# Two narrow products of a two-block transformer kernel: block compression by 64-row tiles, and the modulation's sums over partitions by column tiles

## The chip, the cores and the metric

The kernel runs on one core of a Trainium2 chip. The core has five engines with an instruction stream each: TensorE (matmuls), VectorE, ScalarE, GpSimd and SyncE, which here issues nearly all DMAs. The metric is the device time of one launch in microseconds, as the median of several runs.

## The reference, cut to what matters

A sequence of 256 tokens of 1024 channels goes through two layers with a feed-forward part of 16384 experts each, and then through one more block with a modulation and sparse attention. All is float32. Two places matter here.

The third block's modulation is six vectors of 1024 numbers, made from one vector c, so it can be worked out at any time before that block begins:

```python
mod = jax.nn.silu(c) @ ada_w[layer] + ada_b[layer]          # (1, 1024) @ (1024, 6144)
shift1, scale1, gate1, shift2, scale2, gate2 = jnp.split(mod, 6, axis=-1)
u = rms_norm_2(h, norm1_g[layer]) * (1 + scale1) + shift1
```

In its attention, keys and values (two kv heads of 64 channels) are compressed: 15 overlapping blocks of 32 tokens each become one row, through a weight of 2048 x 64 that both heads share.

```python
blk = src[:, idx] + pos[None, None, :, None, :]             # 15 blocks of 32 tokens
blk = blk.transpose(0, 1, 3, 2, 4).reshape(B, nc, NSA_KV_HEADS, CMP_BLOCK * HEAD_DIM)
return jax.nn.silu(blk @ w1) @ w2                           # w1 (2048, 64), w2 (64, 64)
```

The expert part of each layer picks 16 experts for each of 8 heads and token; its second half sums the picked rows of `v` by their gates, here as a dense product of all 16384 rows with coefficients that are mostly zero.

## The kernel before, in words

Each engine's instruction stream is written out by a Python function per stage (`..._sp`, `..._po`, `..._ac`, `..._ve`, `..._pe` for SyncE, GpSimd, ScalarE, VectorE and TensorE), and each engine runs its stream in order. There are five stages: `even`, `peer(0)`, `odd`, `peer(1)` and `last`. Waits name an event (`wait_ge("ada", pc, 3)`), and a small class turns them into semaphore values. PSUM is `PS`, 8 banks of 128 partitions x 512 floats. `emptied[b]` holds the event after which bank b may be written again, and `bank_wait(pe, b)` waits for it. All calls of a kind go through one helper, so every matmul shows as line 170 of the profile, every ScalarE activation as 181, and SBUF tensors mostly carry the name `mem`, since they are slices of one large tensor.

Most weights are split into a rounded high part and a low remainder: ScalarE rounds (`hi`, the rows `r_sh<-mem`), VectorE subtracts (`lo`, `r_sl<-mem,r_sh`), and TensorE makes the products with both. These products have rounded operands and take one instruction each. Products of unrounded float32 operands, the ones of this change among them, take two instructions on TensorE.

The second half of an expert part is a loop over 128 blocks `V[j]` of 128 experts. For each block, TensorE makes twelve products of 512 moving columns into banks 4 to 7. ScalarE rounds the coefficients of block j + 1 (`coef_high`) and its weights (`hi`), VectorE makes the remainders, and SyncE loads tiles of 128 x 1024 into four buffers `raw`. In `peer(0)` alone this loop carries the modulation as well: `ada_w` comes in 12 pieces of 512 columns with four loads each. In the blocks j = 4 + 10 pc + 0, 2, 4, 6 VectorE adds the eight products of `silu(c)` with the rows of piece pc into `ada_sum`, 128 partitions x 512. In block 4 + 10 pc + 8 TensorE sums over the partitions (`modulation_pe`): four products whose weights are 128 columns of `ada_sum` and whose moving operand is one column of ones, so that the 512 sums come out as four columns of 128 partitions. In the next such block VectorE adds the biases and stores them in `mod` (event `mod`).

The stage `last` begins on VectorE with the scales `gs1` and `gs2` from `mod`. TensorE first makes `bias_mm`, a table of relative biases, which ScalarE copies out and SyncE sends to device memory and back; then it makes the input projection block by block (`block_T`, `parts_R`). The first normalized activations reach it by way of a Ln and an Exp on ScalarE and of VectorE's products. After twelve blocks (`N1 + N0`) comes `compress(0)` for the keys, then the groups of the projection for the values of the attention (`parts_R`), and between them `compress(1)` for the values. In `blk` the partitions 0 to 63 hold the channels of kv head 0 and 64 to 127 those of head 1. The weight `cw1` comes as 32 tiles of 128 x 128 with the head's 64 x 64 on the diagonal and zeros elsewhere, so that one product over 128 partitions makes both heads' 64 columns:

```python
for i in range(32):
    m = pe.matmul(PS[0:15, 3 - a, 0:128], blk[:, a, i, :], wi[:, i, :], i == 0, i == 31)
```

ScalarE then applies Silu to the 15 x 128 of each a, and TensorE turns them.

## Time and the profile before

| | |
|---|---|
| median of 3 runs | 2443.44 us (2441.01 to 2444.06) |
| span of the profiled execution | 2439.0 us |
| TensorE busy | 2406.4 us, 99% of the span, 16544 instructions |
| VectorE busy | 1712.0 us, 70% |
| ScalarE busy | 1331.9 us, 55% |
| GpSimd busy | 435.7 us, 18% |
| read from HBM | 415.96 MB, 172 GB/s over the span |

The profiled execution's own time is its span, from its first instruction to its last; the runs are timed from outside and lie 2.0 to 5.1 us above it. In rows of a timeline, "x8" is a run of eight instructions of the same kind, the time is from the first one's start to the last one's end, and the bracket says how long the engine stood idle before and what released it. The form `128*128 128x512` of a matmul is the weights' partitions and columns, then the moving operand's. One float32 product appears as two instructions. The ends of matmuls are modelled, so spacing is read from starts.

### The profile page before, as it was taken

Reading aid. Unit: us, or ns where it says so; the run is one execution under the profiler, and the core shown is the slowest. Engines: PE = TensorE matmul, PEld = TensorE weight load, DVE = VectorE, ACT = ScalarE, POOL = GpSimd, SP = SyncE. Lnnn points to the kernel's source line nnn. Section 1 sums busy time; section 2 is a strip of 40 time slices with the busy share of each in tenths; the row PEclk is TensorE's granted clock in tenths of the full one; section 3 lists DMA queues with packets and bytes.
Section 4 is the critical chain, followed back from the end, with each engine's and each line's share of the span. In section 5 each row is a group of like instructions: output and inputs, shape, how many; then the busy total and the mean of one; then the engine's idle time right before and its main releaser. Section 6 shows DMA issues by size and latency. Waiting matters only on the chain.

```text
span 2439.0 us, 41647 instructions
## 1 busy us (share of the span) xinstructions
PE 2406.4 (99%) x16544; PEld 2213.2 (91%) x16544; DVE 1712.0 (70%) x3247; ACT 1331.9 (55%) x2520; POOL 435.7 (18%) x386
## 2 busy tenths in 40 slices
PE   8999999999999999999999999999999999999999
PEld 8899999999888888888999999998888878889999
DVE  7867998678777777656599977775555564636864
ACT  6665445766544444566544466665454554556643
POOL 4700000788200000010000048850000000001000
PEclk9999999999999999999999999999999999999999
DMA  7233555443677787632255544446555564223452
GB/s 280 75 139 114 184 183 182 135 130 130 210 260 255 263 263 263 247 129 97 99 187 182 183 155 131 130 139 211 195 192 195 192 235 173 104 99 144 173 180 80
DMA packets 93200, 421.82 MB, mean 173 GB/s; under 512 B 10296, under 2 KB 12880, under 8 KB 85072
## 3 DMA queue, kind: packets, MB, share of 16 engines
q1 hardware_dynamic: 92720, 418.82, 50.3%
q8 instruction: 133, 2.18, 0.4%
q14 instruction: 59, 0.48, 0.1%
q10 hardware_dynamic: 288, 0.34, 0.0%
HBM read 415.96 MB, written 3.16 MB: 172 GB/s over the span
## 4 chain that ended last, share of the span: by engine, by line
PE 94%; DVE 3%; ACT 3%; issue 1%; DMA 0%; ACTq 0%; DVEq 0%
PE PS L170 93%; ACT mem L181 1%; ACT r_sh L181 1%; DVE r_sl L191 1%; DVE mem L191 1%; PE PS L173 1%; DVE mem L199 0%; ACT L188 0%; DMA mem<-in_v 0%; DMA cst<-in_cst 0%; DVE mem L211 0%; ACT xT L181 0%; ACT r_hhi L181 0%; ACT L181 0%; DVE xT L191 0%
## 5 line engine op out<-in xcount | busy, mean ns | idle before, releaser
L191 DVE TENSOR_TENSOR r_sl<-mem,r_sh 128x1024 fp32r<-128x1024 f32 (+2 forms) x750 | 895.3, 1194 | 521.5 <-ACT r_sh L181 520.6
L181 ACT ACTIVATE r_sh<-mem 128x1024 fp32r<-128x1024 f32 (+2 forms) x750 | 768.5, 1025 | 524.0 <-PE PS L170 468.0
L170 PE MATMUL PS<-r_hhi,r_sh 128*128 128x256 f32 (+1 forms) x2832 | 718.7, 291 | 6.2 <-ACT r_sh L181 3.2
L170 PE MATMUL PS<-r_hlo,r_sh 128*128 128x256 f32 (+1 forms) x2704 | 667.7, 284 | 1.3 <-DVE r_hlo L199 1.1
L170 PEld LDWEIGHTS PS<-r_hhi,r_sh 128*128 128x128 f32 (+1 forms) x2832 | 542.1, 191 | 16.2 <-issue 9.6
L170 PEld LDWEIGHTS PS<-r_hlo,r_sh 128*128 128x128 f32 (+1 forms) x2704 | 518.0, 192 | 5.9 <-DVE r_hlo L199 3.3
L196 POOL TENSOR_SCALAR xT<-cst,mem 128x128 f32<-128x128 f32 x256 | 327.4, 1290 | 560.3 <-ACT mem L181 498.0
L170 PE MATMUL PS<-r_hhi,r_sl 128*128 128x256 f32 (+1 forms) x2832 | 401.1, 283 | 0.3 <-DVE r_sl L191 0.3
L181 ACT ACTIVATE mem<-PS 128x256 f32<-128x256 f32 (+25 forms) x558 | 186.0, 341 | 339.6 <-PE PS L170 339.1
L170 PEld LDWEIGHTS PS<-r_hhi,r_sl 128*128 128x128 f32 (+1 forms) x2832 | 366.9, 192 | 0.9 <-DVE r_sl L191 0.5
L170 PE MATMUL PS<-r_sh,r_ch 128*128 128x512 f32 x1024 | 276.8, 391 | 1.2 <-ACT r_sh L181 1.2
L170 PE MATMUL PS<-r_sl,r_ch 128*128 128x512 f32 x1024 | 274.9, 389 | 0.0
L170 PE MATMUL PS<-r_sh,r_cl 128*128 128x512 f32 x1024 | 274.8, 389 | 0.0
L170 PEld LDWEIGHTS PS<-r_sh,r_ch 128*128 128x128 f32 x1024 | 190.8, 188 | 42.1 <-ACT r_sh L181 3.1
L170 PEld LDWEIGHTS PS<-r_sl,r_ch 128*128 128x128 f32 x1024 | 192.2, 188 | 40.3
L170 PEld LDWEIGHTS PS<-r_sh,r_cl 128*128 128x128 f32 x1024 | 192.2, 188 | 40.1
L170 PE MATMUL PS<-mem 64*128 64x128 f32 (+9 forms) x886 | 137.7, 308 | 0.3 <-DVE mem L202 0.2
L170 PE MATMUL PS<-xT 128*128 128x128 f32 x1024 | 130.1, 275 | 4.0 <-DVE xT L191 4.0
L170 PEld LDWEIGHTS PS<-mem 64*128 64x128 f32 (+4 forms) x886 | 106.7, 162 | 28.8 <-issue 12.9
L170 PEld LDWEIGHTS PS<-xT 128*128 128x128 f32 x1024 | 122.8, 192 | 4.3 <-issue 4.3
L191 DVE TENSOR_TENSOR r_cl<-mem,r_ch 128x256 fp32r<-128x256 f32 x256 | 107.1, 418 | 2.6 <-ACT r_ch L181 2.6
L181 ACT ACTIVATE mem<-mem 128x256 f32<-128x256 f32 (+6 forms) x153 | 79.9, 531 | 53.2 <-DVE mem L205 49.3
(169 smaller groups left out, 2649.2 us busy)
## 6 DMA issues: line engine op xcount, KB each, us to landing
mem<-in_u SPq DMA_DIRECT2D x256, 512.0 KB, 3.8
mem<-in_v SPq DMA_DIRECT2D x256, 512.0 KB, 4.4
mem<-in_w SPq DMA_DIRECT2D x16, 2048.0 KB, 8.0
mem<-in_ada SPq DMA_DIRECT2D x48, 512.0 KB, 4.2
mem<-in_in SPq DMA_DIRECT2D x9, 2048.0 KB, 8.9
mem<-in_wq SPq DMA_DIRECT2D x8, 2048.0 KB, 8.4
mem<-in_od_in SPq DMA_DIRECT2D x6, 2048.0 KB, 9.4
mem<-in_ev_in SPq DMA_DIRECT2D x5, 2048.0 KB, 13.1
```

Of the source, the lines that this page charges most:

```text
L170: return self.did(self.e and self.e.matmul(out, lhsT, rhs, start=start, stop=stop, skip_group_check=skip))
L173: return self.did(self.e and self.e.transpose(out, in_, identity))
L181: return self.did(self.e and self.e.activation(out, in_, func, **kw))
L191: return self.did(self.e and self.e.tensor_tensor(out, a, b, op))
L196: return self.did(self.e and self.e.tensor_scalar(out, a, s1, s2, op0, op1))
```

## The change

Modulation: the 12 pieces go four at a time. VectorE keeps the sums of four pieces beside each other, in four quarters of a buffer that is free in this loop (`hTf`). Behind every fourth piece TensorE makes four products, now with one column of ones as the weights and the 512 columns of a piece's sums as the moving operand; each goes to a 32-column tile of its own and leaves a row of 512 sums in partition 0, 32, 64 or 96 of a bank. ScalarE, which took no part before, copies the four rows to SBUF and issues four DMAs that write them to a buffer `md` in device memory. At the end of the loads of `odd`, SyncE loads the 6144 numbers back as 48 rows of 128; TensorE turns them to 128 x 48 as its first instructions of `last`, ahead of `bias_mm`, and VectorE adds all biases in one operation and stores `mod`, ahead of `gs1` and `gs2`. ScalarE waits for its last DMAs in `odd`, before it writes there to the buffer that the rows came from.

Compression: for each i there are two products with 64 partitions and 64 columns, one for each head, into two banks (3 - a and 6 + a), in place of one with 128 partitions and 128 columns. The weights in memory stay as they were; the zeros are no longer read. ScalarE applies Silu to each head's 15 x 64 by itself.

```diff
-    ada_sum = small[:, 0:512]
+    ada_sum = [hTf[:, 512 * i:512 * i + 512] for i in range(4)]
+    ada_row, ada_in = small[:, 0:512], small[0:48, 640:768]
...
                     hi(ac, V[j + 1])
+                if j:
+                    modulation_ac(ac, j - 1)
...
+                s = ada_sum[pc % 4]
                 if q == 0:
                     ve.wait_ge("cs", 0)
-                    if pc:
-                        ve.wait_ge("ada_sum", pc - 1)
-                    d = ve.tensor_scalar(ada_sum, r_[:, 0:512], cs[:, 0:1], MUL)
+                    if pc >= 4:
+                        ve.wait_ge("ada_rows", pc // 4 - 1)
+                    d = ve.tensor_scalar(s, r_[:, 0:512], cs[:, 0:1], MUL)
...
-            else:
-                ve.wait_ge("ada_sum", pc)
-                ve.tensor_tensor(mod[:, 4 * pc:4 * pc + 4], PS[:, pc % 4, 0:4], P("adab")[:, 4 * pc:4 * pc + 4], ADD).then_inc("mod", pc)
+
+        def four_pieces(j):
+
+            pc = (j - 4) // 10
+            if layer or j < 4 or pc >= 12 or pc % 4 != 3 or (j - 4) % 10 != 8:
+                return None
+            return pc // 4
 
         def modulation_pe(pe, j):
-            pc = (j - 4) // 10
-            if layer or j < 4 or pc >= 12 or (j - 4) % 10 != 8:
+            g = four_pieces(j)
+            if g is None:
                 return
-            b = pc % 4
-            bank_wait(pe, b)
-            pe.wait_ge("ada", pc, 3)
+            bank_wait(pe, g)
+            pe.wait_ge("ada", 4 * g + 3, 3)
             for m in range(4):
-                last = pe.matmul(PS[:, b, m:m + 1], ada_sum[:, 128 * m:128 * m + 128], ones[:, 0:1], True, True)
-            last.then_inc("ada_sum", pc)
-            emptied[b] = ("mod", pc)
+                last = pe.matmul(PS[32 * m:32 * m + 1, g, :], ones[:, 0:1], ada_sum[m], True, True)
+            last.then_inc("ada_rows", g)
+            emptied[g] = ("ada_row", g, 3)
+
+        def modulation_ac(ac, j):
+            g = four_pieces(j)
+            if g is None:
+                return
+            ac.wait_ge("ada_rows", g)
+            if g:
+                ac.wait_ge("ada_out", g - 1, 3)
+            for m in range(4):
+                d = ac.activation(ada_row[32 * m:32 * m + 1, :], PS[32 * m:32 * m + 1, g, :], COPY).then_inc("ada_row", g, m)
+            ac.wait_ge(*d)
+            for m in range(4):
+                at = 512 * (4 * g + m)
+                ac.dma_start(io["md"][at:at + 512].rearrange("(o n) -> o n", o=1), ada_row[32 * m:32 * m + 1, :]).then_inc("ada_out", g, m)
...
+            sp.wait_ge("ada_out", 2, 3)
+            sp.dma_start(ada_in, io["md"].rearrange("(m n) -> m n", n=128)).then_inc("ada_in", 0)
...
             hi(ac, ns[1])
+            ac.wait_ge("ada_out", 2, 3)
             scale_ac(ac, 2)
...
-                        ac.activation(hid15[0:15, 128 * a:128 * a + 128], PS[0:15, 3 - a, 0:128], ACT.Silu).then_inc("cmpS", a)
+                        ac.activation(hid15[0:15, 128 * a:128 * a + 64], PS[0:15, 3 - a, 0:64], ACT.Silu)
+                        ac.activation(hid15[0:15, 128 * a + 64:128 * a + 128], PS[0:15, 6 + a, 0:64], ACT.Silu).then_inc("cmpS", a)
...
-            ve.wait_ge("mod", 11)
+            ve.wait_ge("ada_turned", 0)
+            ve.wait_ge(*ve.tensor_tensor(mod, PS[:, 7, 0:48], P("adab"), ADD).then_inc("mod", 0))
...
         def last_pe(pe):
+            bank_wait(pe, 7)
+            pe.wait_ge("ada_in", 0)
+            pe.transpose(PS[:, 7, 0:48], ada_in, ident[0:48, 0:48]).then_inc("ada_turned", 0)
+            emptied[7] = ("mod", 0)
             bank_wait(pe, 6)
...
-                bank_wait(pe, 3 - a)
+                heads = ((slice(0, 64), 3 - a), (slice(64, 128), 6 + a))
+                for _, b in heads:
+                    bank_wait(pe, b)
...
                 for i in range(32):
-                    m = pe.matmul(PS[0:15, 3 - a, 0:128], blk[:, a, i, :], wi[:, i, :], i == 0, i == 31)
+                    for rows, b in heads:
+                        m = pe.matmul(PS[0:15, b, 0:64], blk[rows, a, i, :], wi[rows, i, rows], i == 0, i == 31)
                 m.then_inc("cmp", a)
-                emptied[3 - a] = ("cmpS", a)
+                for _, b in heads:
+                    emptied[b] = ("cmpS", a)
```

## Rows read from the trace of the kernel before

**Rows 1.** The page: busy time of the engines, and the chain by line.

```profile
PE 2406.4 (99%) x16544; PEld 2213.2 (91%) x16544; DVE 1712.0 (70%) x3247; ACT 1331.9 (55%) x2520; POOL 435.7 (18%) x386
...
PE PS L170 93%; ACT mem L181 1%; ACT r_sh L181 1%; DVE r_sl L191 1%; DVE mem L191 1%; PE PS L173 1%; DVE mem L199 0%; ACT L188 0%; DMA mem<-in_v 0%; DMA cst<-in_cst 0%; DVE mem L211 0%; ACT xT L181 0%; ACT r_hhi L181 0%; ACT L181 0%; DVE xT L191 0%
```

**Rows 2.** Windows: length; PE, PEld, DVE, ACT, POOL busy; PEclk, DMA share, GB/s.

```profile
633.87:992.49 358.62, 357.80 (x1622) 296.30 (x1621) 262.83 (x365) 174.83 (x256) 0.00 (x0) 1.00 0.79 265
1631.43:1977.61 346.18, 345.77 (x1527) 285.82 (x1525) 199.25 (x257) 174.92 (x256) 0.00 (x0) 1.00 0.61 202
```

**Rows 3.** Timeline of TensorE, first layer's expert sums: start, length, instruction.

```profile
667.99 1.07 PE L170 MATMUL PS<-r_sh,r_ch 128*128 128x512 f32 x4
...
670.72 0.95 PE L170 MATMUL PS<-cst,small 128*128 128x1 f32 x8
671.53 1.17 PE L170 MATMUL PS<-r_sh,r_ch 128*128 128x512 f32 x4
...
674.38 1.07 PE L170 MATMUL PS<-r_sh,r_ch 128*128 128x512 f32 x4
```

**Rows 4.** Chain of waits in the last stage: start, length, what ran.

```profile
1993.06 52.66 PE PS L170 x379
```

**Rows 5.** Timeline of TensorE, last stage, around both compressions.

```profile
2021.86 1.02 PE L170 MATMUL PS<-mem,cst 128*128 128x512 f32 x2
2022.81 7.16 PE L170 MATMUL PS<-mem 128*15 128x128 f32 x64
2029.90 0.40 PE L170 MATMUL PS<-r_sh,r_hhi 128*128 128x280 f32 x1
...
2034.92 7.16 PE L170 MATMUL PS<-mem 128*15 128x128 f32 x64
```

**Rows 6.** Timeline of TensorE: narrow tiles in the first and last stage.

```profile
42.58 1.71 PE L170 MATMUL PS<-mem 64*128 64x128 f32 x16
...
82.63 0.35 PE L170 MATMUL PS<-mem 64*64 64x128 f32 x4
...
2086.45 0.43 PE L170 MATMUL PS<-mem 128*64 128x256 f32 x2
```

**Rows 7.** Window over the 64x64 tiles, of the tile mem alone.

```profile
82.63:83.07 0.44, 0.44 (x16) 0.44 (x18) 0.44 (x2) 0.44 (x3) 0.44 (x1) 1.00 0.00 0
```

**Rows 8.** Groups by line and form, ScalarE: count, busy us, mean ns, idle before.

```profile
L181 ACT ACTIVATE mem<-PS 128x512 f32<-128x512 f32 x8 | 4.6, 590 | 2.0 <-PE PS L170 2.0
...
L181 ACT ACTIVATE mem<-PS 128x64 f32<-128x64 f32 x6 | 1.3, 216 | 0.0
```

**Rows 9.** Timeline of all engines, start of the last stage.

```profile
1986.06 1.22 DVE L191 TENSOR_TENSOR r_sl<-mem,r_sh 128x1024 fp32r<-128x1024 f32 x1
...
1986.75 0.81 PE L170 MATMUL PS<-cst,small 33*8 33x384 f32 x2
...
1988.10 0.34 SPq L229 DMA_DIRECT2D fd<-mem  x1
...
1988.91 1.35 DVE L199 SCALAR_TENSOR_TENSOR hT<-xT,mem,small 128x256 f32<-128x256 f32 x2 [1.63 <-ACT small L181]
```

**Rows 10.** Timeline of ScalarE, first layer's expert sums.

```profile
670.98 1.06 ACT L181 ACTIVATE r_sh<-mem 128x1024 fp32r<-128x1024 f32 x1 [1.36 <-PE PS L170]
...
688.78 1.06 ACT L181 ACTIVATE r_sh<-mem 128x1024 fp32r<-128x1024 f32 x1 [1.90 <-DMA mem<-in_v]
```

**Rows 11.** Timeline of VectorE and ScalarE around the compressions.

```profile
2023.69 0.68 DVE L202 COPY mem<-PS 128x512 f32<-128x512 f32 x1
...
2039.81 0.48 DVE L226 MEMSET mem<- 128x512 f32 x1 [0.17 <-DVE mem L202]
...
2043.94 1.06 ACT L181 ACTIVATE r_sh<-mem 128x1024 fp32r<-128x1024 f32 x1 [0.25 <-PE PS L170]
...
2045.81 0.33 DVE L202 COPY mem<-PS 128x15 f32<-128x15 f32 x2 [5.51 <-PE PS L170]
```

**Rows 12.** Windows at the last stage's start; columns as in rows 2.

```profile
1992.00:1996.00 4.00, 3.74 (x11) 2.73 (x12) 3.72 (x10) 2.37 (x6) 1.99 (x3) 0.50 1.08 319
```

More of the change, by code:

```diff
@@ L283, in declare @@
     io["fd"] = io["fd_t"].ap()
+    io["md_t"] = nc.dram_tensor("md", (12 * 512,), F32, kind="Internal")
+    io["md"] = io["md_t"].ap()
     io["xs"] = nc.dram_tensor("xs", (128, 2048), F32, kind="Internal").ap()
@@ L1591, in modulation_ve @@
                     ve.wait_ge("ada", pc, q - 1)
-                    d = ve.scalar_tensor_tensor(ada_sum, r_[:, 0:512], cs[:, 2 * q:2 * q + 1], ada_sum, MUL, ADD)
+                    d = ve.scalar_tensor_tensor(s, r_[:, 0:512], cs[:, 2 * q:2 * q + 1], s, MUL, ADD)
                 ve.wait_ge(*d.then_inc("dveC"))
-                ve.scalar_tensor_tensor(ada_sum, r_[:, 512:1024], cs[:, 2 * q + 1:2 * q + 2], ada_sum, MUL, ADD).then_inc("ada", pc, q)
-            else:
-                ve.wait_ge("ada_sum", pc)
-                ve.tensor_tensor(mod[:, 4 * pc:4 * pc + 4], PS[:, pc % 4, 0:4], P("adab")[:, 4 * pc:4 * pc + 4], ADD).then_inc("mod", pc)
+                ve.scalar_tensor_tensor(s, r_[:, 512:1024], cs[:, 2 * q + 1:2 * q + 2], s, MUL, ADD).then_inc("ada", pc, q)
```

## The prediction

> **What bounds the kernel now.** I read the page first. TensorE is busy for 99% of the span, and one line of matmuls holds 93% of the chain that ended last [rows 1]; so time taken out of TensorE's stream counts in full, unless another wait ends later at the same place. Then the two stretches that the change touches. The windows of the two expert-sum loops compare themselves: the first layer's, which carries the modulation, took 358.62 us, the second layer's, the same work without it, 346.18 us, 2.72 us for each step from block to block (127 of them) [rows 2]. TensorE's timeline inside the first shows where the difference sits: the block with the eight one-column products behind it takes 3.54 us (667.99 to 671.53), the next one 2.85 us (671.53 to 674.38) [rows 3]. In the last stage the chain of waits is TensorE alone for 52.66 us from 1993.06 on, and both compressions lie in it [rows 4]. In its timeline the two instructions of 512 columns that begin at 2021.86 (1.02 us with the last one's latency, 0.427 us each) have streamed out at about 2022.71; the first compression starts at 2022.81, the block behind it at 2029.90; the second starts at 2034.92 and is as long [rows 5].
>
> **Modulation, removed.** One piece costs TensorE (3.54 − 2.72) + (2.85 − 2.72) = 0.95 us [rows 2, 3]; 12 pieces are 11.4 us, nearly the 12.4 us by which the loops differ. All of it is path. VectorE's 12 small additions and its waits for them go too; it idles there anyway, so I count nothing.
>
> **Modulation, added.** Three groups, each of four fp32 products with one weight column and 512 moving columns. An fp32 product is two instructions (eight for a piece's four products, [rows 3]), and one of 512 columns streams 0.427 us [rows 5], so one piece is 0.86 us. Whether four such streams run together decides the price. The trace has two narrower cases. With 64x64 tiles, four instructions had started by 82.67, 0.04 us after the first, and by 83.07 sixteen of 128 columns [rows 6, 7]; one at a time they would take 16 x 0.109 = 1.74 us, by the pace of [rows 5]. With 128-row, 64-column tiles, which share all rows as the new ones do, two had started within 0.02 us [rows 6]. Four column tiles over all 128 rows are not in the trace. Bounds: 0.86 us a group (all together) to 3.42 us (in turn). I take 0.86: wherever instructions alternate between tiles, the rows show them side by side. To it come a gap of 0.09 us where the tile shape changes (2022.71 to 2022.81, [rows 5]), once in and once out, and the 0.13 us that the block behind loses today: 1.17 us a group, 3.5 us in all. Saved: 7.9 us (bounds 0.2 and 8.5).
>
> ScalarE gets new work in this loop: after each group a wait, four copies of a 1x512 row out of PSUM and four DMA issues. Copies of 512 columns mean 0.59 us [rows 8]; a DMA issue of like size, on SP, took 0.34 us [rows 9]; with 0.2 us for the wait on its own last copy that is 3.9 us. Queued behind it are its roundings of coefficients and weights for two blocks on, then VectorE's remainder of that tile, then TensorE. The two roundings take 1.37 us a block (174.92 us over 128 blocks, [rows 2]). Counted from the end of the last product ahead of the group: the sums reach ScalarE at 1.15 us (until then it rounds a tile anyway, 1.06, [rows 10]), and TensorE wants the later tile at 1.17 + 2 x 2.72 = 6.6 us. So 6.6 − 1.15 − 1.37 = 4.1 us are free; the cover is ScalarE's idle 1.36 us a block [rows 10] and its lead of one block. 3.9 fits, barely: zero. Without that cover I would pay up to 0.5 us a group, 1.5 us. The weight tiles' DMAs, which already end some of ScalarE's waits (688.78, [rows 10]), are held back by as much at most, and have two blocks without a modulation load to catch up. The 24 KB to device memory and 24 KB back are a tenth of one such tile. Behind the last group five blocks, 13.6 us, of the loop are left before the odd stage waits for its DMAs. The load back is one more issue on SP (0.34 us), behind the attention's output weights and ahead of the next query weights, which wait for freed slots anyway: nothing.
>
> **Compression.** Before: 64 instructions of 128 columns, 7.16 us with the last one's latency, 0.109 us apart; from 2022.71 to 2029.90, with a gap at either end, 7.18 us [rows 5]. After: 128 instructions of 64 columns, by turns two for one head on rows 0 to 63 and two for the other on rows 64 to 127. By 0.427 us for 512 columns, 128 would be 107 ns and 64 be 53; with the 2 ns that 109 has over 107, 0.0555 us. If the two row halves overlap, 64 x 0.0555 = 3.55 us, with gaps 3.73, and 3.45 us are saved each time, 6.9 us in all. If they go in turn, 128 x 0.0555 = 7.1 us, and nothing is. The rows lean to overlap: the 64x64 tiles took sixteen instructions in 0.44 us, 27 ns each, the very rate needed here (two in 55 ns) [rows 7]. Where one row half had all eight instructions ahead of the other's, little overlapped: sixteen took 1.71 us [rows 6]; the new loop alternates after two. What no row shows is that rate for more than 24 instructions; the longest steady run of short ones is the compression itself, 64 at 109 ns. So the bounds of a compression are 3.5 and 128 x 0.109 + 0.18 = 14.1 us; I take 3.73, as the burst is of the same kind.
>
> The burst's 27 ns stands against a rule of the Trainium skill, "TensorE: Matmul & The Clock Gate", section "Back-to-back issue gap": with hardware decoding off about 62 ns a matmul bind where the columns are few, otherwise a floor of about 25 ns. The burst agrees with the floor, but is too short to exclude the other. By the burst the whole sum is the −14.5 us below; by 62 ns, an estimate from that page, a compression would be 128 x 0.062 + 0.18 = 8.1 us and the sum −5.7.
>
> New waits there: banks 6 and 7 must be free of the bias tiles 2 and 3. VectorE copies the last of these out from 2023.69, 0.68 us, the one before it earlier still, ahead of the first compression [rows 11]; tile 3 is wanted by the second, then at about 2031.4. No stall. ScalarE makes four Silu calls of 64 columns (some 0.22 each, [rows 8]) in place of two; behind them it now idles 0.25 us before the next tile, at 2043.94 [rows 11]: that covers the 0.2. Who is late next? VectorE's work behind the head norm ends with a memset at 2039.81 + 0.48; its next wait ends at 2045.81, 5.51 us later [rows 11]. The compression takes 3.45 of these, 2 remain. So 6.9 us arrive.
>
> **Start of the last stage.** The turning of the 48x128 rows stands ahead of the bias matmul, which is on the path: it starts at 1986.75, and by way of ScalarE's copy and scale steps VectorE's first product starts at 1988.91 [rows 9]. Eight instructions with 128 weight columns took 0.95 us with latency, 0.1 each [rows 3]; two of these and a gap: +0.3 us. VectorE adds the biases behind it, two small products, and then its 1.22 us remainder [rows 9]; that ends at about 1989.0, under the delayed 1989.2. Bounds 0.1 and 0.7.
>
> **Sum.** −7.9 − 6.9 + 0.3 = −14.5 us on a span of 2439.0, so 2424.5. The runs' median is 4.4 us above that span (time outside the profiled instructions, or a quick run); I carry that: 2443.4 − 14.5 = 2428.9.
>
> **The clock.** TensorE ran at its half level, 1.2 GHz, through 1992 to 1996, behind the wait at the stage's start [rows 12]. The work behind it moves earlier by 8 to 15 us; one such stretch of 4 us more or less is worth half its length, 2 us, either way.
>
> **The rivals.** *Column tiles of full height go in turn.* For it: no row has four. Against: two do overlap. A group costs 3.42 + 0.31 = 3.73, 11.2 in all; only 0.2 saved: −0.2 − 6.9 + 0.3, 2436.6 us. 7%.
>
> *The row halves of the compression go in turn.* For it: the 1.71 us run. Against: alternating instructions. −7.9 + 0.3: 2435.8 us. 4%.
>
> *Instructions are not handed over fast enough* (the slower end). The place is the compression: twice the instructions, half as long. For it: no lasting rate above one in 109 ns, and the 64x64 burst could have been queued beforehand. Against: 27 ns held for sixteen. At 109 ns a compression takes 14.1 in place of 7.18, and the sum is −7.9 + 13.9 + 0.3 = +6.3: 2449.7 us, 4%. The sign turns at 84 ns (7.6 us over two runs are 3.8, and 3.8 + 7.0 = 10.8 over 128). Half way between the two rates, 68 ns: 8.7 + 0.18 = 8.9, 1.7 more each, −7.9 + 3.4 + 0.3: 2439.2 us, 7%. The skill's 62 ns, quoted above, lies beside it.
>
> *ScalarE's new work holds the loop, or a half-clock stretch is added*: 1.5 + 2 us, 2432.4. 4%.
>
> *Forecast*: 74%, own range 2425 to 2432. The three runs differ by 0.12%, and 0.2% (4.9 us) is about what can be told from no change. Faster than that: the forecast and all rivals but the two of the hand-over, 0.89, less 0.01 for waits that I did not see. Same: the half-way rate and that 0.01, 0.08. Slower: 0.04. Range: from the forecast's low end, 2425, to 2437, which takes in both in-turn cases.
>
> **What would show it.** In the profile after: the first loop's window at about 350.7 us, with three stretches of eight instructions of 512 columns and one weight column, about 0.9 us long; each compression 128 instructions in some 3.7 us; ScalarE's copies of 1x512, and no wait of TensorE for ScalarE two blocks on; the last stage's first block 0.3 us later behind its sums. Wrong if the eight instructions take over 3 us, or if the compression's start 60 ns apart or more.

## The result, and the profile after

The change made the kernel faster: 2426.73 us as the median of 4 runs (2424.63 to 2429.40) against 2442.94 us for the kernel before in the same session, a ratio of 0.9937 with a 95% interval of 0.9926 to 0.9949, or 12.5 to 18.1 us. The same kernel in two more sessions gave 13.5 and 14.9 us less (runs 1 and 12 below). One execution of run 3 (3919.51 us, at a granted clock of 0.556) is left out of that run's numbers. The forecast was 14.5 us less, 2428.9 us.

The profiled execution has a span of 2427.6 us, 11.4 less than before. The page of the profile after, busy time and chain, answers to [rows 1]; TensorE still holds nearly all of it:

```profile
PE 2395.0 (99%) x16601; PEld 2199.7 (91%) x16601; DVE 1712.3 (71%) x3236; ACT 1338.9 (55%) x2534; POOL 436.0 (18%) x386
...
PE PS L170 92%; ACT mem L181 1%; ACT r_sh L181 1%; DVE r_sl L191 1%; DVE mem L191 1%; PE PS L173 1%; DMA mem<-in_v 1%; DVE mem L199 0%; ACT L188 0%; DVE mem L211 0%; DVE hT L199 0%; DMA cst<-in_cst 0%; ACT xT L181 0%; ACT r_hhi L181 0%; ACT L181 0%
```

One share in the second line has risen: a DMA of the expert weights (`in_v`), from 0% to 1% of the chain. The windows of the two expert-sum loops, as in [rows 2]: the first fell from 358.62 to 352.14 us, the second did not move.

```profile
631.78:983.92 352.14, 350.77 (x1550) 285.36 (x1549) 263.24 (x353) 181.50 (x268) 0.00 (x0) 1.00 0.79 270
1624.44:1970.61 346.17, 345.76 (x1526) 285.81 (x1525) 199.24 (x257) 174.92 (x256) 0.00 (x0) 1.00 0.61 202
```

TensorE's timeline around the first of the three groups, as in [rows 3]. The block that begins at 747.83 lasts until 751.61, 3.78 us, and the next 2.85, so a group costs (3.78 − 2.72) + (2.85 − 2.72) = 1.19 us. (The blocks with the second and the third group take 3.91 and 3.92 us in this profile and 3.78 in run 1; before each of them ScalarE had waited for a weight transfer.)

```profile
747.83 1.07 PE L170 MATMUL PS<-r_sh,r_ch 128*128 128x512 f32 x4
...
750.64 1.04 PE L170 MATMUL PS<-hT,cst 128*1 128x512 f32 x8
751.61 1.20 PE L170 MATMUL PS<-r_sh,r_ch 128*128 128x512 f32 x4
...
754.46 1.07 PE L170 MATMUL PS<-r_sh,r_ch 128*128 128x512 f32 x4
```

ScalarE's timeline behind it: four copies, four DMA issues, and two roundings without a pause to catch up:

```profile
751.77 2.42 ACT L181 ACTIVATE small<-PS 1x512 f32<-1x512 f32 x4
754.22 1.35 ACTq L229 DMA_DIRECT2D md<-small  x4
755.62 0.42 ACT L181 ACTIVATE r_ch<-mem 128x256 fp32r<-128x256 f32 x1 [1.43 <-issue]
755.94 1.04 ACT L181 ACTIVATE r_sh<-mem 128x1024 fp32r<-128x1024 f32 x1
```

TensorE's timeline in the last stage, as in [rows 5]: each compression is now 128 instructions, and 3.68 us lie between its first start and the block behind it (2016.54 to 2020.22), where it was 7.09:

```profile
2015.58 1.02 PE L170 MATMUL PS<-mem,cst 128*128 128x512 f32 x2
2016.54 3.75 PE L170 MATMUL PS<-mem 64*15 64x64 f32 x128
2020.22 0.40 PE L170 MATMUL PS<-r_sh,r_hhi 128*128 128x280 f32 x1
...
2025.25 3.75 PE L170 MATMUL PS<-mem 64*15 64x64 f32 x128
```

VectorE's timeline behind the compressions: its wait for TensorE, 5.51 us in [rows 11], is down to 2.11:

```profile
2030.15 0.48 DVE L226 MEMSET mem<- 128x512 f32 x1 [0.17 <-DVE mem L202]
2032.74 0.33 DVE L202 COPY mem<-PS 128x15 f32<-128x15 f32 x2 [2.11 <-PE PS L170]
```

And TensorE's timeline at the last stage's start, as in [rows 9]. From the last block of the second loop to the first block here are 1983.27 − 1970.61 = 12.66 us, against 1990.08 − 1977.61 = 12.47 before: the turning costs 0.19.

```profile
1979.75 0.26 PE L173 MATMUL PS<-cst,small 48*128 48x48 f32 x1
1979.94 0.81 PE L170 MATMUL PS<-cst,small 33*8 33x384 f32 x2
1983.27 0.55 PE L170 MATMUL PS<-r_hhi,r_sh 128*128 128x256 f32 x1 [2.53 <-ACT r_hhi L181]
```

So the profiled execution's 11.4 us come apart as follows. The first loop gave 6.48, the compressions (from the start of the first to the end of the second: 19.20 before, 12.39 after) 6.81, and the last stage's start took 0.19: 13.1 us for the change itself. Where the code is the same, 1.7 us were lost again: 2.09 won ahead of the first loop, and 1.58 lost between the two loops, 0.54 between the last stage's first block and the first compression, and 1.66 behind the second. The first experiment is about these.

### The profile page after: what moved, and what is told of

Read it like the earlier page. It is cut to its first block, busy times and chain, and to the rows that moved or that the text cites. A ratio compares the mean times of both kernels' runs of the same rounds, so it can differ in the third digit from the quotient of the medians.

```text
span 2427.6 us, 41773 instructions
## 1 busy us (share of the span) xinstructions
PE 2395.0 (99%) x16601; PEld 2199.7 (91%) x16601; DVE 1712.3 (71%) x3236; ACT 1338.9 (55%) x2534; POOL 436.0 (18%) x386
## 4 chain that ended last, share of the span: by engine, by line
PE 93%; DVE 3%; ACT 3%; DMA 1%; issue 1%; ACTq 0%; DVEq 0%
PE PS L170 92%; ACT mem L181 1%; ACT r_sh L181 1%; DVE r_sl L191 1%; DVE mem L191 1%; PE PS L173 1%; DMA mem<-in_v 1%; DVE mem L199 0%; ACT L188 0%; DVE mem L211 0%; DVE hT L199 0%; DMA cst<-in_cst 0%; ACT xT L181 0%; ACT r_hhi L181 0%; ACT L181 0%
## 5 line engine op out<-in xcount | busy, mean ns | idle before, releaser
L181 ACT ACTIVATE mem<-PS 128x256 f32<-128x256 f32 (+27 forms) x560 | 186.1, 340 | 339.0 <-PE PS L170 338.5
L170 PE MATMUL PS<-mem 128*64 128x128 f32 (+7 forms) x1014 | 132.9, 291 | 0.3 <-DVE mem L202 0.2
L170 PEld LDWEIGHTS PS<-mem 128*64 128x64 f32 (+4 forms) x1014 | 103.6, 155 | 27.3 <-issue 12.9
```

What stands on the lines that cost most here:

```text
L170: return self.did(self.e and self.e.matmul(out, lhsT, rhs, start=start, stop=stop, skip_group_check=skip))
L181: return self.did(self.e and self.e.activation(out, in_, func, **kw))
```

## The experiments

**1. The change once more.** No edit.

> The changed kernel once more, unchanged, to see which of its differences from before come back. What the change does itself must come back: the first loop's window at 352 us (352.14 in the first profile), each compression 128 instructions in 3.75 us, the last stage's first block 0.3 us later behind its sums. What is chance in one execution should not: the stretches at TensorE's half level (after: 118 to 126 at 0.79, 1425 to 1430 at 0.66, 2050 to 2056 at 0.54) and the 2.0 us that the first profile gained ahead of the first loop. Theory: the time is 2424 to 2430 us, 13 to 18 below before, and the profiled spans of two executions differ by 1 to 3 us by the half-level stretches alone. Rival (the change itself brings the stretch at 1425 to 1430): it comes back at the same place with the same 1.4 us.

Measured: 2429.11 us (5 runs; before 2442.62), ratio 0.9948 (0.9933 to 0.9963). The first group, the compressions and the stage's start were the same to 0.02 us; the loop took 351.35 us. Two windows of this run, the loop and the place of the first profile's half-level stretch:

```profile
632.32:983.67 351.35, 349.77 (x1550) 285.67 (x1549) 263.82 (x353) 181.85 (x268) 0.00 (x0) 1.00 0.80 271
1425.00:1430.00 5.00, 5.00 (x45) 5.00 (x45) 3.66 (x7) 2.47 (x9) 4.23 (x4) 1.00 0.57 194
```

The same place in the first profile after, where TensorE was granted 0.66 and got through 31 matmuls in these 5 us, not 45:

```profile
1425.00:1430.00 5.00, 5.00 (x31) 5.00 (x31) 4.14 (x8) 2.05 (x6) 3.93 (x4) 0.66 0.61 203
```

The stretch did not come back, and the time between the two loops was 638.9 us, as in the kernel before. In a third profile of the change (run 12) it was there again, with 640.5. So the change does not bring it every time, and the rival falls as it was put. Of the twelve profiles with the changed loop five show 640.4 to 640.5 there (the first one and runs 3, 6, 8 and 12); the two with the old loop show 638.9. That is too few to say whether the shift in time makes it likelier. Behind the second compression it is alike: up to the last matmul 394.2 us in the kernel before and in runs 4 to 6, 395.8 in the first profile after and in run 12, 397.4 in this run. Such stretches are worth up to 3 us at one place in one execution, which is why spans and medians can't be compared to the microsecond, and windows can.

**2 and 3. One part alone.** Run 2 is the kernel before with the new `compress` and the new Silu calls; run 3 is the changed kernel with the old ones, in its core:

```diff
-                    for rows, b in heads:
-                        m = pe.matmul(PS[0:15, b, 0:64], blk[rows, a, i, :], wi[rows, i, rows], i == 0, i == 31)
+                    m = pe.matmul(PS[0:15, 3 - a, 0:128], blk[:, a, i, :], wi[:, i, :], i == 0, i == 31)
```

> The kernel before with the compression's part of the change alone. Theory (the two parts add up, each on the path): the first loop's window stays at 358.6 us, each compression's 128 instructions take 3.75 us in place of 7.16, so 6.8 us less than before: a ratio of 0.9972. Rival (part of the gain is given back behind the compressions, to VectorE's work or to a wait of TensorE for ScalarE's Silu): the block behind the second compression comes 6.8 us earlier, but the one at the end of the values' projection less than 5 us earlier, ratio above 0.998.

> The changed kernel with the compression put back to the 64 instructions of 128 columns. Theory (the two parts add up): the first loop's window at 352 us, compressions at 7.16 us, the last stage's first block 0.3 us later behind its sums: 6.1 us less than before by these stretches, ratio 0.9975; with the compression alone it makes up the whole change. By the predicted sum (loop 350.7) it would be 7.6 less, ratio 0.9969. Rival (the modulation brings more than its loop shows, since the runs' medians differ by 16.2 us where the profiled stretches give 13): 9 us less or more, ratio 0.9963 or below.

Measured: the compression alone 2434.01 us, ratio 0.9964 (0.9954 to 0.9974), 6.4 to 11.2 us less; the modulation alone 2433.16 us, ratio 0.9962 (0.9948 to 0.9976), 5.9 to 12.7 us less. In their profiles the parts are where they were expected. With the compression alone the loop is 358.02 us, and TensorE's timeline has

```profile
2020.84 3.75 PE L170 MATMUL PS<-mem 64*15 64x64 f32 x128
...
2029.55 3.75 PE L170 MATMUL PS<-mem 64*15 64x64 f32 x128
```

From the first of these to the block behind the second run 2 takes 12.39 us, as the whole change does, and the wait of VectorE stays open: nothing is given back there, and the rival of run 2 falls. With the modulation alone the loop is 351.97 us and the compressions are at 7.16. Its ratio lies where its own rival put it (0.9963 or below), and its interval takes in the theory's 0.9975 as well. Its stretches give 6.7 us less in the loop and 0.2 more at the stage's start, so by the windows the two parts add up. By the runs it stays open: the two ratios are 0.36% and 0.38% below one, the whole change, run beside them, 0.52%.

**4. Head after head.**

```diff
-                for i in range(32):
-                    for rows, b in heads:
+                for rows, b in heads:
+                    for i in range(32):
```

> The changed kernel with the two loops of a compression exchanged: all 32 products of head 0 (rows 0 to 63), then all 32 of head 1 (rows 64 to 127); the same 128 instructions, operands and banks. Theory (two row halves run side by side only where instructions of both stand close to each other in the queue): 128 instructions one after the other at 55.5 ns, 7.1 us each, 7.3 with latency, so both give back 3.5 us each: 7.0 us slower than the change, as before in the compression. Rival (the halves overlap in whatever order they come): 3.75 us each and no difference. Second rival (64 columns of one half can't follow each other every 55 ns, since the next weights are loaded on the same rows): 109 ns each, 14 us a compression, 20 us slower than the change.

Measured: 2435.35 us, ratio 0.9969 (0.9958 to 0.9980), in the session in which the change had 0.9948. TensorE's timeline:

```profile
2015.23 7.11 PE L170 MATMUL PS<-mem 64*15 64x64 f32 x128
...
2027.29 7.11 PE L170 MATMUL PS<-mem 64*15 64x64 f32 x128
```

This is the theory: 7.04 us from the first start to the block behind, 3.36 more than in the change, each time. All of the compression's gain comes from two row halves that stream at the same time. The zeros that are no longer multiplied are worth nothing by themselves, since 128 times 55 ns is 64 times 110.

**5. Column tiles made full width.**

```diff
-                last = pe.matmul(PS[32 * m:32 * m + 1, g, :], ones[:, 0:1], ada_sum[m], True, True)
+                last = pe.matmul(PS[:, m, :], ones, ada_sum[m], True, True)
```

> The changed kernel with the modulation's products over the full width: the weights are 128 columns of ones in place of one, so that each of the four pieces fills all 128 partitions of a bank of its own (banks 0 to 3), and ScalarE copies one row of each bank. The same eight instructions of 512 columns a group, the same copies and DMAs. Theory (the gain of the modulation is four column tiles that stream side by side): the eight instructions go in turn, 8 x 0.427 = 3.42 us a group in place of 0.86, the block with the group takes 6.34 us in place of 3.78, and the loop is 7.7 us longer, 359 us: the modulation's gain is gone. Rival (the gain is that one column is weighed in place of 512, and tiles play no part): the block stays at 3.8 us and the time at the change's 2427 to 2429.

Measured: 2433.64 us, ratio 0.9966 (0.9954 to 0.9979). The loop's window, and TensorE's timeline at the first group:

```profile
634.03:992.11 358.08, 356.63 (x1550) 290.24 (x1549) 263.63 (x353) 181.91 (x268) 0.00 (x0) 1.00 0.79 267
```

```profile
750.34 1.07 PE L170 MATMUL PS<-r_sh,r_ch 128*128 128x512 f32 x4
...
753.06 3.59 PE L170 MATMUL PS<-hT,cst 128*128 128x512 f32 x8
756.09 1.48 PE L170 MATMUL PS<-r_sh,r_ch 128*128 128x512 f32 x4
...
759.23 1.07 PE L170 MATMUL PS<-r_sh,r_ch 128*128 128x512 f32 x4
```

The eight instructions start 0.43 us apart, one behind the other, and the two blocks (750.34 to 759.23) take 8.89 us, where the change's (747.83 to 754.46) take 6.63. That is 2.26 us a group, 6.8 in all, and with them nearly all of the modulation's gain is gone. It is 0.3 a group less than expected; 0.18 of that are the two gaps where the tile shape changes, which products of their neighbours' shape don't have. The rival falls: a product with one weight column is no cheaper than one with 128, but four of them run side by side.

**6. ScalarE's copies twice.**

```diff
+            for m in range(4):
+                d = ac.activation(ada_row[32 * m:32 * m + 1, :], PS[32 * m:32 * m + 1, g, :], COPY).then_inc("ada_twice", g, m)
+            ac.wait_ge(*d)
```

> The changed kernel with each of the four rows copied twice by ScalarE, one round of four behind the other: 2.4 us more of ScalarE in each of the three groups, and nothing else. Theory (ScalarE's 3.8 us just fit between the group and the roundings that TensorE wants two blocks later, with 0.2 us to spare): TensorE stands 2.2 us in each group's third block, 6.6 us more in the loop, which is then about 358 us. Rival (ScalarE has at least another block of lead, so the cover was never tight): under 0.5 us a group, the loop at 351 to 352.5 us.

Measured: 2435.74 us, ratio 0.9972 (0.9962 to 0.9982); the loop is 357.37 us. ScalarE's timeline, then TensorE's, at the first group:

```profile
750.76 4.88 ACT L181 ACTIVATE small<-PS 1x512 f32<-1x512 f32 x8
```

```profile
755.27 1.07 PE L170 MATMUL PS<-r_sl,r_ch 128*128 128x512 f32 x4
758.49 1.19 PE L170 MATMUL PS<-r_sh,r_ch 128*128 128x512 f32 x4 [2.15 <-ACT r_sh L181]
```

TensorE stands for ScalarE's rounding, and the three blocks concerned take 5.03, 4.95 and 4.96 us in place of 2.72, so 2.2 to 2.3 us more for 2.46 us of new work (4.88 against 2.42). The cover had about 0.2 us left, as the theory says; one more copy of 0.59 us would, by that, have cost most of its length (an estimate).

**7. A quarter of the modulation's bytes.** Three quarters of each modulation tile are not loaded, so the modulation's numbers are others.

```diff
-                sp.dma_start(raw[i % 4], src).then_inc(f"raw{i % 4}", layer, i)
+                n = 256 if i in ada.values() and layer == 0 else 1024
+                sp.dma_start(raw[i % 4][:, 0:n], src[:, 0:n]).then_inc(f"raw{i % 4}", layer, i)
```

> The changed kernel with only the first 256 of 1024 columns of each modulation load (128 KB in place of 512 KB; the rest of the tile keeps older values, so the modulation's numbers are not the reference's). All instructions of the engines are the same. In the change's two profiles the loop is 346.17 us (the second layer's) plus three groups of 1.19 us, 349.7, plus 1.6 to 2.4 us in blocks that are longer elsewhere. Theory (those blocks wait for weight tiles whose transfers are late, because the loop carries the same bytes in less time): with a quarter of the modulation's bytes no block outside the groups is longer than 2.78 us except the loop's first two, and the loop is 349.7 to 350.0 us. Rival (they come from ScalarE's copies and DMA issues, or from the order of SP's queue): the loop stays at 351.3 to 352.2 us with long blocks at the same places.

Measured: 2425.39 us in one run. The loop's window, and the group of ScalarE's weight roundings in it (count, busy us, mean ns, then the idle time ahead of them by what ended it):

```profile
631.83:981.61 349.78, 349.37 (x1550) 285.89 (x1549) 260.82 (x353) 181.94 (x268) 0.00 (x0) 1.00 0.68 218
```

```profile
L181 ACT ACTIVATE r_sh<-mem 128x1024 fp32r<-128x1024 f32 x127 | 134.6, 1060 | 162.1 <-PE PS L170 156.3 <-DMA mem<-in_v 5.8
```

The same group in the first profile after, and in the kernel before:

```profile
L181 ACT ACTIVATE r_sh<-mem 128x1024 fp32r<-128x1024 f32 x127 | 134.6, 1060 | 164.9 <-PE PS L170 87.8 <-DMA mem<-in_v 76.7
```

```profile
L181 ACT ACTIVATE r_sh<-mem 128x1024 fp32r<-128x1024 f32 x127 | 134.7, 1060 | 182.2 <-PE PS L170 128.9 <-DMA mem<-in_v 53.2
```

Outside the groups and the loop's first two blocks none is longer than 2.78 us any more, and the loop is 346.17 + 3 x 1.19 us to 0.04. ScalarE's waits that a weight transfer ended fall from 76.7 us to 5.8. They are 53.2 in the loop of the kernel before (54.3 in run 2, which has the old loop too), and 70.4 to 82.9 in every profile that has the changed loop and the full loads. So the longer blocks wait for weights that come late, and late they come because of the modulation's bytes, not through ScalarE's new work.

The other half of the theory, that they are late because the loop has less time for the same bytes, is not shown: this run changes the bytes, not the time. And the longest of these blocks in the three profiles of the change stands where the time is the same. It is block j = 9, ahead of the first product of the modulation in either kernel (block 12 before, 42 after). TensorE's timeline at its end, in the kernel before and then in run 1:

```profile
662.38 1.21 PE L170 MATMUL PS<-r_sh,r_ch 128*128 128x512 f32 x4 [0.42 <-ACT r_sh L181]
```

```profile
661.58 1.19 PE L170 MATMUL PS<-r_sh,r_ch 128*128 128x512 f32 x4 [1.18 <-ACT r_sh L181]
```

It takes 3.30 us in the kernel before (659.08 to 662.38), 2.94 in run 2, and from 2.72 (run 6) to 4.05 (run 1, 657.53 to 661.58) with the changed loop and the full loads. In each of the two profiles ScalarE's rounding had waited over 3 us for its weight transfer. In run 1 this one block holds 1.3 of the 1.6 us of longer blocks.

**8. Four tiles in the compression.** The odd half of the sums is left out behind it.

```diff
-                        m = pe.matmul(PS[0:15, b, 0:64], blk[rows, a, i, :], wi[rows, i, rows], i == 0, i == 31)
+                        o = 64 * (i % 2)
+                        m = pe.matmul(PS[o:o + 15, b, 0:64], blk[rows, a, i, :], wi[rows, i, rows], i < 2, i >= 30)
```

> The changed kernel with the compression over four tiles in place of two: of each head's 32 products the even ones go to output partitions 0 to 14 and the odd ones to partitions 64 to 78 of the same bank, so that two streams run on each row half. The same 128 instructions; the odd half of the sums is left out behind it, so the output is not the reference's. Theory (the rate of 27 to 28 ns an instruction, which the change's compression and the 64x64 tiles of the trace of before both show, is how fast instructions start): the compression stays at 3.5 us. Rival (that rate was two row halves, each streaming 64 columns in 55 ns): four tiles take half, 1.8 us a compression, 14 ns an instruction, and 3.7 us fall off the time in all.

Measured: 2423.94 us in one run. TensorE's timeline:

```profile
2014.58 1.98 PE L170 MATMUL PS<-mem 64*15 64x64 f32 x128
...
2021.52 1.98 PE L170 MATMUL PS<-mem 64*15 64x64 f32 x128
```

The theory falls and the rival is right: 128 instructions lie within 1.76 us from the first start to the last, 14 ns each. The 27 ns of the change are no limit on starting instructions; they are 55 ns of streaming on each of two row halves.

**9. Coarser turns.**

```diff
-                for i in range(32):
-                    for rows, b in heads:
-                        m = pe.matmul(PS[0:15, b, 0:64], blk[rows, a, i, :], wi[rows, i, rows], i == 0, i == 31)
+                n = 4 if a else 2
+                for first in range(0, 32, n):
+                    for rows, b in heads:
+                        for i in range(first, first + n):
+                            m = pe.matmul(PS[0:15, b, 0:64], blk[rows, a, i, :], wi[rows, i, rows], i == 0, i == 31)
```

> The changed kernel with coarser turns between the heads: in the keys' compression two products (four instructions) of one head and then two of the other, in the values' compression four products (eight instructions) each. Same instructions, operands and banks. Known: in turns of one product (two instructions) 3.53 us from first to last start, in turns of 32 products 6.89 us. Theory (TensorE starts an instruction for a free row half past some, but not many, that wait for the other half): turns of four still overlap nearly whole, 3.5 to 4.5 us, turns of eight mostly not, 5.5 to 6.9, like the sixteen in turns of eight of the first stage before, 1.71 us. Rival A (it looks far ahead): 3.5 us in both. Rival B (it only looks past one product): about 6 us or more already in turns of four.

Measured: 2429.52 us in one run. TensorE's timeline, with turns of four instructions and then of eight:

```profile
2014.75 3.76 PE L170 MATMUL PS<-mem 64*15 64x64 f32 x128
...
2023.46 4.19 PE L170 MATMUL PS<-mem 64*15 64x64 f32 x128
```

Turns of four cost nothing (3.54 us from first to last start), turns of eight 0.45 us (3.98). Started strictly in order, with 55 ns for each instruction on its row half, they would take about 5.3 and 6.2 us (an estimate: 32 turns of three steps, 16 of seven; the change's own turns of two come to 3.5 either way). So the theory falls for turns of eight, and rival A is nearest: TensorE takes instructions for a free row half past several that wait for the other half. Why the sixteen narrow products of the first stage [rows 6], eight and eight, ran in turn then, stays open. Their 128 moving columns alone are not the reason: the 64x64 tiles of [rows 6, 7] have as many and also come eight for one row half and then eight for the other, and there four instructions had started by 0.04 us and sixteen within 0.44. What no run here separates is the 128 weight columns.

**10. Keys and values at once, and the turning moved back.** The core of it; Silu and the turning of the hidden rows follow to partitions 64 a to 64 a + 14:

```diff
+                for i in range(32):
+                    for a in range(2):
+                        for rows, b in heads:
+                            m = pe.matmul(PS[64 * a:64 * a + 15, b, 0:64], blk[rows, a, i, :], wi[a][rows, i, rows], i == 0, i == 31)
...
+            lo(ve, N1[0])
             ve.wait_ge("ada_turned", 0)
```

> A version meant to be complete: the changed kernel with both compressions made at once at the first one's place, over four tiles: rows by head as in the change, keys to output partitions 0 to 14 and values to 64 to 78 of one bank per head, 256 instructions by turns; and the turning of the modulation's rows moved behind the bias matmul, with VectorE's remainder ahead of the bias addition. Theory (four tiles of 64 columns start every 14 ns; the first block's delay is the turning alone): 3.5 us for all 256, where the change takes 3.7 twice, and the last stage's first block 0.3 us earlier behind its sums than in the change: 4.0 us less than the change, 2423 to 2425 us, ratio to before 0.9925. Rival (256 instructions are more than can be handed over at that rate, which the 128 of the earlier run drew from a queue that had filled): 7 us for the 256 or more, and no gain over the change. Second rival (the values' weights or VectorE's blocks are not there at the earlier place): a wait of TensorE for them ahead of the compression of 1 us or more.

Measured: 2428.78 us, ratio 0.9951 (0.9937 to 0.9965), no gain over the change. TensorE's timeline, and then the chain of waits behind it:

```profile
2015.77 2.18 PE L170 MATMUL PS<-mem 64*15 64x64 f32 x138
2018.49 1.86 PE L170 MATMUL PS<-mem 64*15 64x64 f32 x118 [0.54 <-issue]
2020.28 0.40 PE L170 MATMUL PS<-r_sh,r_hhi 128*128 128x280 f32 x1
```

```profile
2021.71 0.41 issue
...
2025.98 0.70 ACT mem L181
...
2027.86 1.29 DVE mem L199
...
2031.60 6.04 PE PS L170 x32
```

After 138 of the 256 instructions TensorE stood for 0.54 us with no wait for another engine, and again for 0.41 behind them. The 256 took 4.51 us (2015.77 to 2020.28), between the theory's 3.5 and the first rival's 7; what TensorE waited for in these gaps no view shows. No wait stands ahead of the compression, so the second rival falls. And without the values' compression behind the head norm, the chain from 2025.98 to 2031.60 runs over ScalarE and VectorE, where in run 1 it is TensorE alone from 2004.91 to 2030.62:

```profile
2004.91 25.70 PE PS L170 x370
```

That compression had been the cover for their work. The other part failed as well. The bias matmul did start 0.19 us earlier behind the sums, but VectorE's first product now began together with GpSimd's (VectorE's timeline, then GpSimd's),

```profile
1981.14 1.44 DVE L199 SCALAR_TENSOR_TENSOR hT<-xT,mem,small 128x256 f32<-128x256 f32 x2 [0.65 <-ACT small L181]
```

```profile
1981.17 0.72 POOL L191 TENSOR_TENSOR hT<-xT,small 128x256 f32<-128x256 f32 x1 [366.43 <-ACT small L181]
```

and took 1.04 us of the 1.44 for its two, where in run 1 it took 0.48 and began 0.11 us ahead of GpSimd's. The stage's first block came 13.09 us behind the sums (1969.77 to 1982.86), in run 1 12.66. The Trainium skill, "GPSIMD Engine Reference", section "1. Specifications", says that the two engines share their interface to SBUF, with contention for VectorE instructions that read two inputs there; the 0.48 and 1.04 us agree with that. Why the two began together here is not settled.

**11 and 12. Half of both at each place, beside the change.** Each visit makes 16 of the 32 products, for keys and values, in the same banks; the stage's start is the change's. Run 12 is the change without an edit.

```diff
-                for i in range(32):
+                for i in range(16 * half, 16 * half + 16):
```

> A complete version again, with what the last run taught: the changed kernel with four tiles in both compressions, each of which now makes half of the 32 products for the keys and the values together (keys to output partitions 0 to 14, values to 64 to 78 of one bank per head), and the second goes on in the same banks; 128 instructions at each of the two old places. The start of the last stage is the change's own. Theory (at 128 instructions a visit TensorE does not outrun its queue, and the second visit still covers the work of ScalarE and VectorE behind the head norm): each visit takes 1.9 us, no wait appears behind the second, and the block behind it stands 3.5 us earlier than in the change, counted from the last stage's first block; 3.5 us less than the change beside it, which is 0.14%. Rival (the cover behind the second visit is used up: in the change VectorE's wait there was 2.1 us long, and both visits shorten by 1.8): VectorE or ScalarE end last behind the head norm and at least 1 us of it is given back. Second rival (the keys' weights are held until the second visit, and the projection weights that take their slot come late): a wait of TensorE or ScalarE for a transfer later in the stage.

> The changed kernel unchanged, on the chip of the run above, so that the two can be compared in the same session. Both theories: 2425 to 2430 us; by the first theory of the run above 3.5 us more than that, by the rivals 1 to 3 us more.

Measured: two visits 2426.04 us, ratio 0.9931 (0.9916 to 0.9946); the change beside it 2427.24 us, ratio 0.9935 (0.9920 to 0.9950). TensorE's timeline of run 11:

```profile
2013.61 1.98 PE L170 MATMUL PS<-mem 64*15 64x64 f32 x128
...
2020.54 1.98 PE L170 MATMUL PS<-mem 64*15 64x64 f32 x128
```

From the last stage's first block to the turning of the hidden rows run 11 takes 45.50 us (1980.24 to 2025.74) and run 12 49.04 (1983.28 to 2032.32): the 3.5 us of the theory, without a new wait, and both rivals fall. The median is only 1.2 us lower, and the intervals overlap. In the profiled execution TensorE at its half level took 3.0 us back behind the compressions: the 30 products of the first row below take 4.31 us in run 12 (from 2043.64), and the granted clock from 2040 to 2048 was 0.71 (the chain of waits of run 11, then a window).

```profile
2037.07 7.32 PE PS L170 x30
```

```profile
2040.00:2048.00 8.00, 7.94 (x51) 7.68 (x50) 2.27 (x8) 2.69 (x7) 0.00 (x0) 0.71 0.71 258
```

Run 11 is the best complete version found, by 3.5 us in its windows; its runs do not separate it from the change.

## Why the prediction was right, point by point

**What bounds the kernel.** Right: what TensorE's stream lost in its windows arrived at the end, up to the half-level stretches.

**Modulation, removed and added.** 11.4 us out and 3.5 us in were forecast; a group measures 1.19 us, where 1.17 was worked out. That four column tiles stream side by side, which no row of before showed, is right, and run 5 shows that it is the tiles that do it; in turn they cost 2.26 us more a group. That rival had 7%.

**The loop's sum** is the term that was mis-sized. The forecast was 7.9 us; three profiles of the change gave 6.5, 7.3 and 6.4 (352.14, 351.35 and 352.25 us), and six more with the same loop (runs 3, 4 and 8 to 11) 6.7 to 7.9 (351.97 to 350.75). The up to 1.5 us that are missing belong to none of the costed instructions. The kernel before already had 358.62 − 346.18 − 11.4 = 1.0 us of blocks that were longer for other reasons, and the step took these as given; with the changed loop they are 1.0 to 2.5. Run 7 names what they wait for: weight transfers that come late because of the modulation's bytes, and the DMAs that end some of ScalarE's waits [rows 10] do so for longer in the changed loop (70.4 to 82.9 us, not 53.2). The prediction priced how much ScalarE's new work delays these loads, and gave them two blocks to catch up; it did not ask how late they come, and how differently from one execution to the next, without it. Whether the shorter loop makes them later stays open: the block that varies most, j = 9, lies ahead of everything that got shorter.

**ScalarE's new work.** 3.9 us were forecast and 3.8 measured (751.77 to 755.57); the block concerned took 2.74 us in place of 2.72. So zero was right, and "fits, barely" too: run 6 found about 0.2 us of cover left.

**Compression.** 3.45 us each were forecast and 3.41 measured. The bet on the rate of a burst of sixteen [rows 7] held over 128 instructions, and run 4 shows that the overlap of the row halves is all of it. That the two rates agree is a coincidence: the burst was four tiles at 109 ns each, the compression is two row halves at 55, and run 8 shows that 27 ns is no limit of its own. One reading was wrong: that little overlaps where one row half has eight instructions ahead of the other's. The 64x64 tiles that did overlap come eight and eight for the row halves as well, and run 9 lost only 0.45 us by such turns. It cost nothing, since the change alternates after two. The page that spoke against it, the Trainium skill's "TensorE: Matmul & The Clock Gate", section "Back-to-back issue gap", has about 62 ns a matmul with hardware decoding off, and a floor of about 25 ns otherwise. Run 8 differs from both, with 14 ns an instruction over four tiles, and the measurement decides. The sum by 62 ns, −5.7 us, lies 7.3 to 8.2 us from the 13.0 to 13.9 that the windows of the change give.

**Who is late next.** VectorE's wait behind the compressions was to keep 2 us; it kept 2.11. Run 10 shows what it is worth.

**The turning.** 0.3 us were forecast and 0.19 measured.

**The clock.** It was named with 2 us either way, and the stretches took 1.7 us net in the first profile. That is why its span fell by 11.4 us while the windows of the three profiles give 13.0 to 13.9 for the change itself, and the medians of the three sessions 13.5 to 16.2. That the forecast's 14.5 lies in the middle of these is in part luck: by the windows alone it was 0.6 to 1.5 us too much.

## What to carry to other kernels

Narrow float32 products gain from tiles when instructions of different tiles lie close to each other in the stream: two row halves in turns of up to four instructions ran at twice the rate, and four column tiles in turns of two at some three and a half times (eight instructions in 0.97 us, where in turn they start 0.43 us apart), while head after head gained nothing. A loop that waits for some transfers differs by itself from one execution to the next (here by up to 1.5 us for the same instructions), so take several profiles of it before and after. And a short product that is moved may have been what covers another engine at its old place; look for the next wait there first.

## What the runs showed that was not expected

Four tiles with 64 moving columns started an instruction every 14 ns over 128 of them (run 8), while with 256 in one go TensorE stood for 0.54 us after 138 (run 10). Turns of eight instructions between the row halves cost only 0.45 us in 3.5 (run 9). And stretches of TensorE's clock at its half level came and went at the same places of the same code: between the two loops 638.9 or 640.5 us, behind the compressions 394.2, 395.8 or 397.4. The blocks of the first expert-sum loop that wait for late weights vary as much: one block took 2.72 to 4.05 us with the same instructions ahead of it.
